# First attention of a ten-part transformer kernel: a new order of input slots, heads and output slots

## What is computed

```python
shift, scale, gate = ada_modulation(c, ada_w[0, 0], ada_b[0, 0])   # silu(c) @ w + b
h = x * (1.0 + scale) + shift
qkv = h @ w_in                                    # 8 query heads, 2 key and 2 value heads of 128
q, k = partial_rope(q, cos, sin), partial_rope(k, cos, sin)
scores = q @ k.T * 128 ** -0.5, masked to |qpos - kpos| <= 128
m = maximum(max(scores), sink); p = exp(scores - m)
o = (p / (sum(p) + exp(sink - m))) @ v
x = layer_norm(ALPHA * x + (1.0 + gate) * (o @ w_out))
```

## Time and profile before

| | us |
|---|---|
| median of 3 runs | 2263.32 |
| runs | 2262.86 to 2265.74 |
| profiled execution, from first to last instruction | 2263.8 |
| PE busy | 2168.8 (96%) |
| DVE busy | 1559.0 (69%) |
| ACT busy | 1133.0 (50%) |
| chain that ended last: PE, DVE, ACT | 74%, 15%, 5% |

### The profile page before, as it was taken

How to read it: one execution, slowest core, us unless ns; L and a number is a source line. 1 busy time by engine, 2 the same in 40 slices (tenths; PEclk the granted TensorE clock), 3 DMA queues, 4 the chain that set the end, 5 groups by cost and what they waited for, 6 DMA issues and landing times.

```text
span 2263.8 us, 36177 instructions
## 1 busy us (share of the span) xinstructions
PE 2168.8 (96%) x15272; PEld 1997.2 (88%) x15272; DVE 1559.0 (69%) x1871; ACT 1133.0 (50%) x1500; POOL 352.8 (16%) x306
## 2 busy tenths in 40 slices
PE   4889999999999999999999999999999999999998
PEld 4668998887899899999899899999999988998997
DVE  6888897698755754569865774465456996757545
ACT  2344444796544443456664453344345767445342
POOL 2112324331110210030021140022003001112000
PEclk9899999999999999999999999999999999999999
DMA  9749894444365455665442465546566554235552
GB/s 358 240 143 333 300 329 152 119 115 126 133 215 191 157 198 187 166 190 150 122 118 70 149 205 183 181 149 220 185 182 168 154 136 112 94 124 183 194 189 93
DMA packets 304982, 396.96 MB, mean 175 GB/s; under 512 B 48032, under 2 KB 263706, under 8 KB 304821
## 3 DMA queue, kind: packets, MB, share of 16 engines
q1 hardware_dynamic: 285440, 336.75, 46.5%
q0 software_dynamic: 18496, 57.59, 8.1%
q10 hardware_dynamic: 884, 0.30, 0.1%
HBM read 393.53 MB, written 1.07 MB: 174 GB/s over the span
## 4 chain that ended last, share of the span: by engine, by line
PE 74%; DVE 15%; ACT 5%; issue 3%; DMA 1%; POOL 0%; SPq 0%; DVEq 0%; ACTq 0%; POOLq 0%
PE tiles L522 15%; PE tiles L523 15%; PE tiles L524 15%; PE y_rows L522 7%; PE y_rows L523 7%; PE y_rows L524 7%; DVE weights_lo L1439 4%; PE tiles L935 2%; ACT weights_hi L1053 2%; DVE ada_acc L1487 2%; DMA ada_ring<-in_ada_w_dram 1%; ACT xt L1090 1%; PE tiles L653 1%; PE tiles L629 1%; DVE rnn_gates L1769 1%
## 5 line engine op out<-in xcount | busy, mean ns | idle before, releaser
L1439 DVE TENSOR_TENSOR weights_lo<-weights_raw,weights_hi 128x2048 fp32r<-128x2048 f32 (+2 forms) x316 | 765.5, 2431 | 433.2 <-ACT weights_hi L1053 432.5
L522 PE MATMUL tiles<-xt_hi,weights_hi 128*128 128x256 f32 (+1 forms) x3200 | 911.6, 285 | 16.1 <-ACT xt L1090 7.0
L523 PE MATMUL tiles<-xt_lo,weights_hi 128*128 128x256 f32 (+1 forms) x3200 | 905.8, 283 | 0.0
L524 PE MATMUL tiles<-xt_hi,weights_lo 128*128 128x256 f32 (+1 forms) x3200 | 905.8, 283 | 0.0
L1053 ACT ACTIVATE weights_hi<-weights_raw 128x2048 fp32r<-128x2048 f32 (+2 forms) x316 | 592.3, 1878 | 218.0 <-PE y_rows L524 165.7
L522 PEld LDWEIGHTS tiles<-xt_hi,weights_hi 128*128 128x128 f32 (+1 forms) x3200 | 607.2, 190 | 31.9 <-issue 24.6
L523 PEld LDWEIGHTS tiles<-xt_lo,weights_hi 128*128 128x128 f32 (+1 forms) x3200 | 607.5, 190 | 2.7
L524 PEld LDWEIGHTS tiles<-xt_hi,weights_lo 128*128 128x128 f32 (+1 forms) x3200 | 607.4, 190 | 0.0
L522 PE MATMUL y_rows<-weights_hi,hid_hi 128*128 128x512 f32 x608 | 239.4, 394 | 0.5 <-DVE weights_lo L1439 0.5
L523 PE MATMUL y_rows<-weights_lo,hid_hi 128*128 128x512 f32 x608 | 237.8, 391 | 0.0
L524 PE MATMUL y_rows<-weights_hi,hid_lo 128*128 128x512 f32 x608 | 237.4, 390 | 0.0
(11 more groups left out here) (367 smaller groups left out, 2767.4 us busy)
## 6 DMA issues: line engine op xcount, KB each, us to landing
weights_raw<-in_ffn_w_dram SPq DMA_DIRECT2D x132, 1024.0 KB, 5.0
weights_raw<-in_mlp_w_dram SPq DMA_DIRECT2D x64, 1024.0 KB, 6.1
weights_raw<-in_w_in_dram SPq DMA_DIRECT2D x52, 1024.0 KB, 5.2
ada_ring<-in_ada_w_dram POOLq DMA_DIRECT2D x76, 512.0 KB, 5.3
weights_raw<-in_rnn_w_in_dram SPq DMA_DIRECT2D x16, 768.0 KB, 4.8
weights_raw<-in_w_in_dram SPq DMA_DIRECT2D x32, 256.0 KB, 4.3
weights_raw<-in_w_branch_a_dram SPq DMA_DIRECT2D x32, 256.0 KB, 4.8
weights_raw<-in_w_branch_b_dram SPq DMA_DIRECT2D x8, 1024.0 KB, 5.2
```

What stands on the lines that cost most here:

```text
L522: pe.matmul(o, a, c, start=first, stop=False)
L523: pe.matmul(o, a, d, start=False, stop=False)
L524: return pe.matmul(o, b, c, start=False, stop=last)
L1439: dve.tensor_tensor(slot_view(WLO, m, NSPL), slot_view(RAW, m, NRAW), slot_view(WHI, m, NSPL).bitcast(F32), ALU.subtract).then_inc(*inc("l ...
```

## The change

1. The six input slots are computed in the order keys, values, queries (`FIRST_SLOTS = (4, 5, 0, 1, 2, 3)`); `plan()` loads them in it too. Labels keep their old numbers.
2. The rope of the keys follows the value slot; that of query slot r follows query slot r + 1, that of slot 3 comes after the turns of heads 0 and 1. `scores1(h)` waits for the rope of its own query slot only, and the scores of heads 0 and 1 stand beneath query slot 3 (the sixth slot), those of heads 2 and 3 behind it. The scratch of the rope moves to where the gate rows will lie.
3. From there heads go in pairs, written out: turns, mixes and scores. Heads 4 to 7 turn and mix in the rotating banks instead of Y (`IN_Y = 4`).
4. Output slot 0 stands between the turns and mixes of heads 4 and 5, output slot 1 between the turns and mixes of heads 6 and 7; slots 2 and 3 (`rows_tail`) follow.
5. On DVE the chunks are placed anew: to 26 among the input slots, 27 behind the second pair copy, to 31 behind norm1 of heads 6 and 7, to 39 in one row ahead of the split that output slot 3 needs, 40 to 43 ahead of the norm as before. The gate rows move behind the turns of heads 6 and 7.

```diff
+FIRST_SLOTS = (4, 5, 0, 1, 2, 3)
+IN_Y = 4
...
-        RTMP = put("rope_tmp", [32, 2, 512], at=a + 12 * KB)
+        RTMP = put("rope_tmp", [32, 2, 512], at=gate_at)
...
-                    for i in range(6):
+                    for i in FIRST_SLOTS:
...
@@ TensorE
             def scores1(h):
-                pe.wait_ge(*past("rope_ready", 4))
+                pe.wait_ge(*past("rope_ready", h // 2))
...
-                if h >= 2:
+                if 2 <= h < IN_Y:
                     pe.wait_ge(*past("free_A", ("pt", h - 2)))
-                bank = y_bank(h % 2)
+                bank = y_bank(h % 2) if h < IN_Y else topen(("pt", h), "A")
...
-                    if h >= 4:
-                        pe.wait_ge(*past("free_D", ("o", h // 2 - 2)))
-                    pair["bank"] = y_bank(2 + h // 2 % 2)
+                    pair["bank"] = y_bank(2 + h // 2 % 2) if h < IN_Y else topen(("o", h // 2), "D")
...
+            for n, i in enumerate(FIRST_SLOTS):
+                if i < 5:
+                    cols_slot((0, "in", i), XH, XL, "A", ready=xready(0) if n == 0 else None)
+                else:
+                    v_slot((0, "in", 5), XH, XL)
+                if n == 1:
+                    pe.wait_ge(*past("const_in"))
+                    rope1(4)
+                if n in (2, 3):
+                    for q in ((0, 2, 3, 4) if n == 2 else (5, 6, 7)):
+                        params(q)
+                if n >= 3:
+                    rope1(n - 3)
+                if n >= 4:
+                    two(scores1, 2 * (n - 4))
+            two(turn1, 0)
+            rope1(3)
             pe.wait_ge(*past("free_A", (0, "in", 5)))
-            for h in range(NH1 + 3):
...
-            pe.wait_ge(*past("free_D", ("o", 3)))
-            for i in range(2):
-                if i == 1:
-                    ada_reduce(4)
-                rows_slot((0, "out", i), lambda k: OH[:, k, :], lambda k: OL[:, k, :], 2 * i, i == 0)
+            two(mix1, 0)
+            two(scores1, 4)
+            two(turn1, 2)
+            two(mix1, 2)
+            two(scores1, 6)
+            ada_reduce(2)
+            two(turn1, 4)
...
+            pe.wait_ge(*past("free_D", ("o", 1)))
+            rows_slot(*out1(0), True)
+            two(mix1, 4)
+            two(turn1, 6)
+            ada_reduce(3)
+            gate_rows(0)
+            rows_slot(*out1(1), False)
+            two(mix1, 6)
+            ada_reduce(4)
+            pe.wait_ge(*past("free_D", ("o", 2)))
+            rows_tail(0, out1(2), out1(3), lambda: pe.wait_ge(*past("free_D", ("o", 3))))
@@ ScalarE
+            for n, i in enumerate(FIRST_SLOTS):
...
                 step((0, "in", i))
+                if n == 5:
+                    two(exp1, 0)
                 dst = QT[:, 2 * i:2 * i + 2, :] if i < 4 else (KT if i == 4 else VR)[:, :, :]
                 evac((0, "in", i), dst, src=pair_of(tile((0, "in", i))))
...
+            two(exp1, 2)
+            two(probs1, 0)
+            two(exp1, 4)
+            heads1(0)
+            two(probs1, 2)
+            two(exp1, 6)
+            heads1(1)
+            two(probs1, 4)
+            step((0, "out", 0))
+            heads1(2)
+            two(probs1, 6)
+            gate_rows(0)
+            step((0, "out", 1))
+            heads1(3)
+            for i in (2, 3):
                 step((0, "out", i))
@@ VectorE
+            for n, i in enumerate(FIRST_SLOTS):
+                step((0, "in", i))
+                if n == 5:
+                    two(norm1, 0)
+                if n == 1:
+                    rope1(4)
...
+                if n >= 3:
+                    rope1(n - 3)
+                if n >= 4:
+                    two(maxima1, 2 * (n - 4))
+                if n < 5:
+                    ada_upto(18 + 2 * n)
+            two(norm1, 2)
+            rope1(3)
+            two(maxima1, 4)
+            heads1(0)
+            two(norm1, 4)
+            two(maxima1, 6)
+            heads1(1)
+            ada_upto(27)
+            modulation(2)
+            two(norm1, 6)
+            ada_upto(31)
+            step((0, "out", 0))
+            heads1(2)
+            modulation(3)
+            ada_upto(39)
+            step((0, "out", 1))
+            heads1(3)
+            modulation(4)
+            for i in (2, 3):
                 step((0, "out", i))
-                if i == 1:
-                    modulation(4)
                 ada_upto(40 + i)
```

More of the change, by code:

```diff
@@ L672, in _, with rope1 @@
                 prep(0, t)
[L675 to L679, removed]
-                if i == 1:
[L681 to L690, removed]
+            def rope1(r):
+                pe.wait_ge(*past("free_A", (0, "in", r)))
+                src = QT[0:32, 2 * r:2 * r + 2, :] if r < 4 else KT[0:32, :, :]
+                bank = topen(("rot", r), "D")
+                pe.matmul(bank[0:32, :], ROT[:, :], src.rearrange("p a b -> p (a b)"), start=True, stop=True).then_inc(*inc("tile_done", ("rot", r)))
             def scores1(h):
-                pe.wait_ge(*past("rope_ready", 4))
+                pe.wait_ge(*past("rope_ready", h // 2))
                 bank = topen(("sc", h), "D")
@@ L725, in mix1, with two @@
                     ins.then_inc(*inc("mix_half", h))
+            def two(f, h):
+                f(h)
+                f(h + 1)
             pair = {}
-            pe.wait_ge(*past("free_A", (0, "in", 5)))
-            for h in range(NH1 + 3):
[L730 to L739, removed]
@@ L1120, in _, with exp1, probs1, heads1 @@
             prep_rest(0)
-            for i in range(6):
-                if i == 3:
+            def exp1(g):
+                act.wait_ge(*past("neg_max", g))
+                for b in range(2):
+                    act.activation(PR[:, g, b, :], PR[:, g, b, :], ACT.Exp, bias=AT1[:, 1, 2 * g + b:2 * g + b + 1],
+                                       accum_out=AT1[:, 2, 2 * g + b:2 * g + b + 1]).then_inc(*inc("p_exp_part", (g, b)))
+                act.activation(AT1[:, 3, 2 * g:2 * g + 2], AT1[:, 1, 2 * g:2 * g + 2], ACT.Exp,
+                                   bias=SNK[:, g:g + 1]).then_inc(*inc("p_exp", g))
+            def probs1(h):
+                bank = y_bank(h % 2) if h < IN_Y else tile(("pt", h))
+                act.wait_ge(*past("tile_done", ("pt", h)))
+                evac(("pt", h), PTB[:, h % 2, :, :], src=bank.rearrange("p (a b) -> p a b", a=4))
+            def heads1(i):
+                bank = y_bank(2 + i % 2) if 2 * i < IN_Y else tile(("o", i))
+                act.wait_ge(*past("tile_done", ("o", i)))
+                act.activation(OH[:, 2 * i:2 * i + 2, :], pair_of(bank), ACT.Copy).then_inc(*inc("oh_ready", (0, i)))
+            def two(f, h):
+                f(h)
+                f(h + 1)
+            for n, i in enumerate(FIRST_SLOTS):
+                if n == 3:
                     act.wait_ge(*past("const_in"))
@@ L1576, in norm1 @@
                     dve.tensor_scalar(PR[:, h, b, :], PR[:, h, b, :], AT1[:, 5, 2 * h + b:2 * h + b + 1], None, ALU.mult).then_inc(*inc("probs_ready", h))
[L1578 to L1596, removed]
@@ L1597, in _, with heads1, two @@
-            for i in range(4):
+            def heads1(i):
+                bank = y_bank(2 + i % 2) if 2 * i < IN_Y else tile(("o", i))
+                dve.wait_ge(*past("oh_ready", (0, i)))
+                dve.tensor_tensor(OL[:, 2 * i:2 * i + 2, :], pair_of(bank), OH[:, 2 * i:2 * i + 2, :].bitcast(F32),
+                                      ALU.subtract).then_inc(*inc("free_D", ("o", i)))
+            def two(f, h):
+                f(h)
+                f(h + 1)
+            for n, i in enumerate(FIRST_SLOTS):
[4 more added lines that the diff above has]
+                    rope1(4)
+                if n in (2, 3):
+                    for q in ((0, 2, 3, 4) if n == 2 else (5, 6, 7)):
+                        params(q)
+                if n >= 3:
[4 more added lines that the diff above has]
+                    ada_upto(18 + 2 * n)
```

34 lines of the change are left out of this document (18 added, 16 removed).

## The result

| | kernel before | changed kernel |
|---|---|---|
| median, us | 2263.91 (20 runs, 2262.44 to 2265.98) | 2267.66 (20 runs, 2263.57 to 2269.43) |
| ratio | | 1.0015, 95% interval 1.0009 to 1.0022 |
| profiled span, us | 2263.8 | 2266.4 |
| norm 0 begins, us from the first matmul of the first input slot | 151.67 - 42.48 = 109.19 | 155.52 - 42.08 = 113.44 |
| from there to the first MLP split, us | 169.67 - 151.67 = 18.00 | 172.36 - 155.52 = 16.84 |

The change costs 3.75 us in the medians: less than 0.2%, but clear of the noise. In the two profiles the norm begins 4.25 us later and lasts 1.16 us less; 0.4 us lies ahead of the stage, which the change does not touch, and what follows the norm is shifted as a whole. 4.25 - 1.16 - 0.4 = 2.7, against 2.6 in the spans. A profile shows one execution.

The account below looks back on a forecast made before the run. VectorE, 89.4 of 107.8 us busy, was taken to bound the stage up to the norm. Walk -1.7 became +0.7 with the clock; the norm's +0.8 made +1.5 on median 2263.32: 2264.8 us, range 2258 to 2269.5.

Parts of the forecast that it names:

- the slower rival: TensorE's clock falls again among the heads, half clock lasting to 117 us: +3.9 to +5.1, taken as 2269 us; chance 0.18.
- its first step: Up to the norm, VectorE's 89.4 us of work stay; only its 18.4 us of idle time can be won.
- The walk: Each engine's instructions laid end to end in the new order: norm at 148.9 against 150.6 us at full clock, -1.7.
- scores 4: VectorE's pause among the heads for these scores, 2.7 us, coming 2.4 us later through the fallen clock.
- the pair copies: VectorE pauses among the heads while ScalarE does two exponentials and the pair copy: 1.9 us, twice.
- signs named for being right: VectorE idle about 18 us, output slot 0 at 115 to 118 us, norm's first x_rows at 151 to 153, among others.
- One fall of the clock: TensorE among the heads at half clock from 96 to 103 us; norm at 151.3 against 150.6, +0.7.
- scores 6: VectorE's pause among the heads for these scores: 0.8 us.
- The tail of TensorE that needs them is not late enough to matter.: Behind the row of eight chunks: tail's first half ends at 145.6 to 148.0, VectorE's last chunk at 149.0 to 151.4.
- Chunk 36: In VectorE's row of eight chunks: a 1.3 us wait, issue at 129.8, landing at 135.0, VectorE free at 133.9.
- The norm, +0.8: TensorE idle some 5 us inside the norm, so its eight transposes run at half clock: +0.8 us (bounds 0 and 1.1).
- The faster rival: Most of VectorE's 9 us of pauses after 97 us close; norm some 7 us earlier, 2256.5 us; chance 0.20.

Follow-up runs that it names:

- e7: Kernel before with only the change's slot order and ropes (keys and values first, scores waiting for their own slot's rope): 2264.07 us, ratio 0.9999.
- e1: Changed kernel with unneeded matmuls filling TensorE's four pauses, order and waits kept: 2265.51 us, ratio 1.0005 to the kernel before.
- e4: Changed kernel with the reduction that waits for chunk 39 moved behind the first part of output slot 2: 2267.58 us, ratio 1.0015 to the kernel before.
- e3: Changed kernel with chunks 27 to 30 placed one by one in VectorE's four waits among the heads: 2266.82 us, ratio 1.0012 to the kernel before.
- e5: e2 with unneeded matmuls in TensorE's two remaining pauses, ahead of output slot 0 and the reduction: 2258.23 us, ratio 0.9975 to the kernel before.
- e2: Changed kernel with only ScalarE's list reordered, copies of turned heads and pair copies ahead of later exponentials: 2259.23 us, ratio 0.9978 to the kernel before.
- e8: e5 with 32 more unneeded matmuls in TensorE's pause inside the norm: 2258.28 us, ratio 0.9974 to the kernel before.

## Why the prediction was right, and where its steps were wrong

The forecast was no change by the bound of 0.2%, on the slow side, +1.5 us; measured +3.75, which is inside the range and under 0.2%, but clear of the noise, and at 2267.66 nearer to the slower rival (2269) than to the forecast (2264.8). The range held it because that rival was in it. It stands on its first step, which held: VectorE's work is conserved (90.00 us against 89.38) and it sets the norm's start. The walk's other early numbers held too: TensorE's wait ahead of the first mix 5.5 us forecast and 5.31 measured, VectorE's for scores 4 2.7 and 2.55, for the pair copies 1.9 each and 1.82 each; the clock was back at 101.6 us. That early scores bring next to nothing fits e7's result. Of the signs named for being right, three were missed: VectorE idle about 18 us (22.0), output slot 0 at 115 to 118 us (118.42), the norm at 151 to 153 (155.52).

Four terms were mis-sized, and they partly cancel. That cancelling is luck: had the norm grown by the 0.8 us forecast instead of shrinking by 1.16, the median would be near 2269.6, just above the range.
- *One fall of the clock.* There were four. The second, behind the pause of 3.88 us, made the wait for scores 6 2.55 us instead of 0.8; in e1, where that pause is filled, it is 0.86. This is the slower rival's first half, and the norm's start (+4.25) lies in the rival's bounds (+3.9 to +5.1). Its mechanism did not come as written, a half clock lasting from 96 to 117 us: the clock was up again between the falls (1.00 from 112 to 118), yet output slot 0 did start at half clock, at 118.4 us behind a pause of 2.4. Filling the four pauses (e1) moved the norm's start by 4.4 us, with two falls still there.
- *"The tail of TensorE that needs them is not late enough to matter."* This step did not hold. The first half of the tail was to end at 145.6 to 148.0 and ended at 155.5. The wait for chunk 39 stands in TensorE's list ahead of the tail. It idled 4.24 us there, the clock fell, the reduction took 3.58 us, modulation 4 waited 0.87 for it, and the tail's first half ended 0.18 us behind VectorE's last chunk. That makes 0.87 + 0.18 us on VectorE's path, and in e4, with the reduction moved, the norm began 1.0 us earlier. I had named what is queued behind the row of eight on VectorE, not the whole tail on TensorE.
- *Chunk 36.* 1.3 us forecast (135.0 - 133.9, the walk's own numbers, give 1.1), 2.91 measured. I took 5.2 us from issue to landing. The DMA engines stood still among the heads, because chunks 27 to 30 were not used there, and all loads then came at once:
```profile
96.00:118.00 22.00, 14.59 (x64) 12.14 (x64) 12.31 (x31) 9.30 (x32) 0.00 (x0) 0.79 0.00 0
...
131.00:138.00 7.00, 7.00 (x38) 5.97 (x37) 3.86 (x4) 3.00 (x3) 2.11 (x4) 1.00 1.02 348
```
  That load took 6.8 us at a DMA share of 1.02, against a median of 4.7. Where e3 used those chunks among the heads, the waits for the ring were 1.68 us.
- *The norm, +0.8.* It was -1.16. I had expected a pause of 5 us inside it, from a tail that ends early. The tail ended late, TensorE paused 1.17 us, the transposes ran at full clock (1.11) and VectorE's wait of 1.24 was gone. A late tail is partly paid back by a shorter norm, and the other way round in e1, e4 and e5.

In sums: VectorE's pauses from 96 us on were to be 9.1 us and are 0.43 + 2.55 + 1.82 + 2.55 + 1.82 + 2.91 + 0.87 = 12.95. That is 3.9 more, which with the walk's +0.7 gives 4.6 for the norm's start, measured 4.25.

One sum of the prediction mixes its bases: the forecast adds to the median 2263.32, the slower rival's 2268.5 to 2269.7 to the span 2263.8; on the median it is 2268.0 to 2269.2.

The faster rival was priced at 7 us earlier, with the remark that the two waits for the pair copies are "fixed by the written order". They are, and that is where the gain lay: reversing two kinds of entries in one list (e2) won 8.4 us against the changed kernel.

What is open: how the 3.75 us divide between clock and order, since no run keeps the clock up throughout, and how often each fall happens over many executions. The change's runs spread over 5.9 us, those of before over 3.5.

## What to carry over

When one engine's work is conserved, a reordering can only win its pauses; walk all engines' lists with the durations of the trace and add up that engine's pauses. Look in every list for an instruction whose data is ready but which stands behind a wait for something later: here copies behind exponentials, worth 8.4 us, where the output slots between the heads are worth 4.6 and the early scores nothing that could be told. And when work is moved, look at what stands behind each wait on *every* engine's list, and count for TensorE the clock behind each new pause as well as the pause.

## What was not expected of the hardware

Pauses as short as 2.4 and 2.5 us were enough for a fall here (ahead of output slot 0: clock 0.68 in 118 to 120 and 0.50 in 120 to 122; before, behind the pause of 2.52 us in the norm), while 2.8 us among the last heads of the kernel before, with matmuls on both sides of it, were not. In e1 the clock fell at 143.4 us with no pause marked in TensorE's timeline since 126.8: 24 unneeded matmuls up to 140.3, the sixteen one-column matmuls of the reduction (1.95 us), and the tail's first matmuls came before it. In e5 and e8 it fell at 106.3 and 105.0 us, behind pauses under 1 us each. The length of the pause alone does not tell.

Nor did TensorE's clock come back equally fast. In the changed kernel, with mixes and scores alone, it is up 4.1 us after the first mix (97.57 to 101.6). In the kernel before TensorE works without a marked pause from 100.05 us, and the clock is 0.50 up to 110; there the first turning is followed by sixteen one-column matmuls that take 3.4 us.
